# A 16-byte tile is allocated later, so that the tiles behind it start 32 bytes lower in the on-chip memory

## What is computed

```python
# first block, four layers: mixers A, B, C, A (diff_attention, latent_attention, dilated_attention)
for i in range(4):
    x = x + mixer[i % 3](rms_norm(x, attn_norm[i]))
    x = x + swiglu(rms_norm(x, ffn_norm[i]), f_w_gu[i], f_w_out[i])   # FFN_DIM 2816
x = rms_norm(x, final_norm)
# in mixer A:
lam = exp(sum(lam_q1 * lam_k1)) - exp(sum(lam_q2 * lam_k2)) + lambda_init
# second block, two layers
h = layer_norm(x, ln_in_g, ln_in_b)
for l in range(2):
    h = layer_norm(ALPHA * h + token_mix(h, ...), ln1_g[l], ln1_b[l])  # pooling, convolution, sparse attention
    h = layer_norm(ALPHA * h + conv_ffn(h, ...), ln2_g[l], ln2_b[l])
```

## Time and profile before

| | |
|---|---|
| median of three executions | 2455.41 us |
| the profiled execution | 2455.41 us |
| its span, first to last instruction | 2453.6 us |
| TensorE matmul busy | 2314.5 us, 94% |
| weight loads busy | 2222.9 us, 91% |
| VectorE busy | 1547.2 us, 63% |
| ScalarE busy | 1138.0 us, 46% |
| GpSimd busy | 345.6 us, 14% |
| mean granted TensorE clock | 0.956 |
| DMA | 362 MB, mean 148 GB/s |

### The profile page before, as it was taken

How to read it: one execution, slowest core, us unless ns; L and a number is a source line. 1 busy time by engine, 2 the same in 40 slices (tenths; PEclk the granted TensorE clock), 3 DMA queues, 4 the chain that set the end, 5 groups by cost and what they waited for, 6 DMA issues and landing times.

```text
span 2453.6 us, 45807 instructions
## 1 busy us (share of the span) xinstructions
PE 2314.5 (94%) x18358; PEld 2222.9 (91%) x18358; DVE 1547.2 (63%) x2028; ACT 1138.0 (46%) x1477; POOL 345.6 (14%) x448
## 2 busy tenths in 40 slices
PE   8899998999999999999989998978999999889998
PEld 8799997699999999999979998977889988868998
DVE  6846547455467776654775554668677557866763
ACT  4643344543345555433564333535355453445552
POOL 0002100012000000220301210660011019100210
PEclk9999998999999999999999999988999999989999
DMA  7327643166544445565533754434346543424651
GB/s 227 122 75 200 188 143 108 45 167 188 187 152 153 142 152 155 160 188 184 179 107 98 194 189 146 130 103 137 103 139 188 189 137 121 161 69 129 189 189 69
DMA packets 431038, 362.12 MB, mean 148 GB/s; under 512 B 20524, under 2 KB 404144, under 8 KB 430904
## 3 DMA queue, kind: packets, MB, share of 16 engines
q1 hardware_dynamic: 429128, 358.79, 48.1%
q0 software_dynamic: 1264, 0.71, 0.1%
q10 hardware_dynamic: 512, 0.72, 0.1%
HBM read 359.12 MB, written 1.05 MB: 147 GB/s over the span
## 4 chain that ended last, share of the span: by engine, by line
PE 80%; DVE 9%; POOL 6%; ACT 3%; issue 1%; DMA 0%; SPq 0%; ACTq 0%; DVEq 0%; POOLq 0%
PE bank L449 70%; POOL hT L1273 4%; DVE weights_lo L1775 3%; POOL Z L1275 2%; PE bank L480 2%; PE bank L552 2%; PE bank L775 1%; PE bank L789 1%; ACT weights_hi L1311 1%; PE bank L687 1%; PE bank L487 1%; PE bank L905 1%; PE bank L937 1%; DVE negmax L1990 1%; PE bank L918 1%
## 5 line engine op out<-in xcount | busy, mean ns | idle before, releaser
L449 PE MATMUL bank<-h_hi,weights_hi 128*128 128x256 f32 (+1 forms) x3856 | 1103.9, 286 | 53.4 <-DVE weights_lo L1775 17.5
L1775 DVE TENSOR_TENSOR weights_lo<-weights,weights_hi 128x2048 fp32r<-128x2048 f32 x343 | 787.9, 2297 | 552.2 <-ACT weights_hi L1311 549.7
L449 PE MATMUL bank<-h_lo,weights_hi 128*128 128x256 f32 (+1 forms) x3856 | 1093.5, 284 | 0.0
L449 PE MATMUL bank<-h_hi,weights_lo 128*128 128x256 f32 (+1 forms) x3856 | 1092.4, 283 | 0.0
L1311 ACT CAST weights_hi<-weights 128x2048 fp32r<-128x2048 f32 x343 | 654.4, 1908 | 560.5 <-PE bank L449 552.2
L449 PEld LDWEIGHTS bank<-h_hi,weights_hi 128*128 128x128 f32 (+1 forms) x3856 | 742.0, 192 | 63.3 <-issue 49.0
L449 PEld LDWEIGHTS bank<-h_lo,weights_hi 128*128 128x128 f32 (+1 forms) x3856 | 742.2, 192 | 1.5 <-issue 1.4
L449 PEld LDWEIGHTS bank<-h_hi,weights_lo 128*128 128x128 f32 (+1 forms) x3856 | 741.3, 192 | 0.0
L449 PE MATMUL bank<-hid_hi,weights_hi 128*128 (+1 forms) x1056 | 296.8, 281 | 0.0
L449 PE MATMUL bank<-hid_hi,weights_lo 128*128 (+1 forms) x1056 | 296.8, 281 | 0.0
L449 PE MATMUL bank<-hid_lo,weights_hi 128*128 (+1 forms) x1056 | 296.8, 281 | 0.0
(11 more groups left out here) (299 smaller groups left out, 2467.7 us busy)
## 6 DMA issues: line engine op xcount, KB each, us to landing
weights<-in_f_w_gu SPq DMA_DIRECT2D x176, 512.0 KB, 5.0
weights<-in_f_w_out SPq DMA_DIRECT2D x88, 512.0 KB, 4.2
weights<-in_w_up SPq DMA_DIRECT2D x88, 512.0 KB, 4.9
weights<-in_w_in SPq DMA_DIRECT2D x82, 512.0 KB, 4.5
weights<-in_c_w_qkv SPq DMA_DIRECT2D x72, 512.0 KB, 4.5
weights<-in_a_w_qkv SPq DMA_DIRECT2D x48, 512.0 KB, 4.6
weights<-in_w_down SPq DMA_DIRECT2D x44, 512.0 KB, 4.2
weights<-in_a_w_o SPq DMA_DIRECT2D x16, 512.0 KB, 4.0
```

What stands on the lines that cost most here:

```text
L449: mm = nc.tensor.matmul(out, x, y, start=(first and n == 0), stop=(last and n == 2), skip_group_check=True)
L1775: v_.tensor_tensor(w_lo[slot][:], raw[slot][:], w_hi[slot][:].bitcast(F32), ALU.subtract).then_inc(lo_ready, 1)
```

## The change

The line that allocates `lams` is moved from before `h_hi` to behind `sign`. No instruction, no loop, no semaphore and no other size is touched, and the order of instructions on each of the five engines is the same.

```diff
--- before.py
+++ after.py
@@ -136,7 +136,6 @@
         w_lo = [sb(f"weights_lo{s}", [P, UNIT], F32R) for s in range(SLOTS)]
         xT = sb("xT", [P, KT, T])
         hT = sb("hT", [P, KT, T])
-        lams = sb("lams", [P, 4])
         h_hi = sb("h_hi", [P, KT, T], F32R)
         h_lo = sb("h_lo", [P, KT, T], F32R)
         sq = sb("sq", [P, KT, T])
@@ -155,6 +154,7 @@
         esum = [sb(f"esum{i}", [P, 2]) for i in range(4)]
         erec = [sb(f"erec{i}", [P, 2]) for i in range(4)]
         sign = sb("sign", [P, 2])
+        lams = sb("lams", [P, 4])
         lame = sb("lame", [P, 4])
         neglam = sb("neglam", [P, 2])
         subg = sb("subg", [P, 2])
```

## The result

The changed kernel takes 2484.26 us (median of four, 2482.19 to 2484.99) against 2453.82 us for the kernel before beside it. The ratio of the fast executions of both is 1.0119, with a 95% interval of 1.0106 to 1.0133; of eleven executions of the changed kernel one was slow, 3246.68 us at a mean granted clock of 0.642, and isn't counted. I had forecast no change, 2455 us, with a range up to 2474.

The account below looks back on a forecast made before the run. The prediction took the distance between L449's matmuls on TensorE as the bound. Its three terms, 0 + 0 + 0 on 2455.41 us, gave 2455 us, no effect beyond 0.3% (chance 0.55), with a range of 2420 to 2474 us.

Parts of the forecast that it names:

- What bounds the kernel: TensorE: time is set by the distance between L449's successive matmuls, 116.7 ns for streamed `h`; weights arrive early.
- `lams` itself: Two instructions touching `lams`, once, beside running products: cost 0, or 0.6 us uncovered and twice as long.
- VectorE, ScalarE and GpSimd: Their instructions on tiles moving by 32 bytes: taken as 0, at most 5 us either way.
- TensorE's reads: Matmuls streaming `h` or holding it stationary: taken as 0, between +19 and -35 us.
- the L552 pair: L552 streams `sq` (remainder 32) and `xT` (remainder 0) over `ones`, both 379 ns: claimed no effect of start.
- The notch is set by something other than the start: `hid` steps differ by up to 3.2 ns on the same tiles and weight slots; claimed to speak against both ends.
- The 16-byte lines: SBUF reads pay per new 16-byte line; both placements start on one, so operands cross as many lines as before.
- The slower rival: L449 with `h`: streamed and loading tiles both at multiples of 64 meet in memory; +19 us, 2474 us; chance 0.20.
- price of 1.8 ns: Weights streamed over stationary `h` at 68 us: 118.5 ns against 116.7, used as the slower rival's cost per step.
- the faster rival: Streamed `h`: the 32-byte remainder costs part of each step; one 3.3 ns notch less, -35 us, 2420 us; chance 0.25.

Follow-up runs that it names:

- e4_rest_alone: Kernel before with unused tiles before `sq` and `lame`: `h` stays, `sq` and the tiles behind it start at a multiple of 64; 2455.97 us, ratio 0.9999.
- e2: Kernel before with `lams` moved before `weights_hi`: weight parts move to remainder 32 by 64, `h` keeps its own remainder 32; 2486.46 us, ratio 1.0134.
- e11: Kernel after with unused tiles of 160 bytes before `h_hi` and 96 before the areas, putting every streamed tile at -96; 2472.17 us, ratio 1.0070.
- e5: The kernel before run once more with a profile, nothing changed; 2457.93 us.
- e12: `h_hi` starts 16 bytes into its tile and `h_lo` 240 into its own, both at +48 from the weights, `hid` at -64; 2461.45 us, ratio 1.0013.
- e3: `h` at a multiple of 64 as in the kernel after, weight parts moved to remainder 32 by unused tiles; 2465.48 us, ratio 1.0043.
- e10: Kernel after with unused tiles of 192 bytes before `h_hi` and 96 before the areas, putting every streamed tile at -64; 2436.75 us, ratio 0.9925.

## Why the prediction was wrong, step by step

**What bounds the kernel: right.** The time is the distance between L449's matmuls, and that alone moved, with nothing new in the waits.

**`lams` itself, 0: not contradicted**, too small to be seen. **VectorE, ScalarE and GpSimd, 0 within 5 us: right.** e4_rest_alone brings every tile that the change moves, `h` apart, to the remainder by 64 of the kernel after, and gives 0.9999. One reading was incomplete: GpSimd's L1273 also reads `pcol` (`hT<-Z,pcol` on the page), which does move; e4 moves it too, so nothing hangs on it.

**TensorE's reads, 0: the step that failed.** I took 0 "by the L552 pair, the only one in the trace that changes the start and nothing else". The runs show 3.3 ns a step in its place, 120.0 after 116.7, some +35 us over the streamed `h`. The pair changes the wrong thing. The start of the streamed tile doesn't set the step, its distance from the loaded one does, as e2 shows with an `h` that never moved. And L552 was no place to see it: before, `sq` stood at distance 0 from `ones` and `xT` at -32, the very pair 120.0 against 118.4 at L449, and both ran 379 ns. Its plain float32 matmuls follow each other after 216 ns (measured between starts, before and after), with loads of 190 ns, so a load beside one has slack; that the slack is what hides the price there is a reading and not tested. After, where both tiles are at 0, it's the same:

```profile
L552 PE MATMUL bank<-sq,ones x96: 379/379/455, 1529.4 to 2465.2; 128*128 128x256 f32 x96
```

**"The notch is set by something other than the start": a half-truth that misled me.** `hid` at 119.9, 118.6 and 117.2 ns is one distance, -96, which has several steps (e11 shows them for `h`, e5 that they can change between executions). I read this as evidence that addresses don't matter. But a distance can fix which steps are possible and leave open which of them a stretch takes.

**The 16-byte lines: the rule didn't hold as a guide to speed.** The Trainium skill's rule (SBUF — State Buffer, Specifications) of a price for each new 16-byte line gives no change, since both starts are on a line. The measurement decides: the same lines, 3.3 ns more a step. e12 shows a distance of 48 to be unlike its neighbours at 32 and 64.

**The slower rival had the place and the two operands right, not the condition and not the size.** The placement of the streamed tile against the loaded one is what counted, at L449, in every product with `h`. That the two readers meet in the memory no trace shows, and equal offsets aren't needed: +96 costs as much as 0. Its price of 1.8 ns came from the earlier trace rows, which I read as the cost of a streamed start at a multiple of 64; it was the cost of -32. The price of 0 is 3.3 ns, 35 us for the 19 I gave. I had that size in hand, as the notch of the faster rival, and put it on one side only. Its condition, agreement by 64, was wrong as well (`h` at +64 costs 1.0 ns, at 128 mostly 1.9).

**The faster rival** was out from the start in its mechanism (e2, e3), but e10 shows that the step can fall by some 3.3 ns, at a distance that the change did not choose. That this is the size it had named is luck.

## What to carry to other kernels

Where matmuls follow each other densely with a fresh full weight load each, compare the placements of streamed and stationary tiles: 32 bytes are worth 1.2% here, and distances of 0 and +96 by 256 are the dear ones in this kernel. To test whether an address matters, move one operand against the other and read the distance between starts in dense stretches; one control that has slack proves nothing. And don't judge a placement by one profile, since at some distances one program has steps of 113 and 118 ns in one execution, and even the kernel before changed some of its steps from one execution to the next.

## What the runs showed of the hardware that I had not expected

- The step of a float32r product of 128 loaded and 256 streamed columns depends on the signed distance of its two operands in the SBUF by 256 bytes: from 113.2 ns (-64, in some stretches) to 120.0 (0, +96) at 2.4 GHz, all with the same instructions.
- What counts is the streamed start less the loaded one, whichever tile has which role: weights over `h` take 118.5 ns at -32, and `h` over weights takes 118.4 at -32 in e3.
- At some distances a stretch falls into one of two or three steps and holds it: 117.3, 118.7 or 120.0 ns at -96, 113.3 or 117.8 at -64 and +64, 116.7 or 117.8 at +32, 118.7 or 120.0 at 128. At 0, +96 and -32 every long stretch had one step. What picks it was not found; in e10 and e11 all `hid` stretches have the step of the `h` stretch before them.
- With two of three matmuls cut to 64 loaded columns and 64 output rows the difference between 0 and +32 is gone, and about 10 ns over the columns remain. Why they do stays open.
